# Moving the activation loads of a one-core transformer trunk from SyncE's queue to GpSimd's

## The chip, the cores and the metric

The kernel runs on one core of one Trainium2 chip, as one launch. The metric is the device time of that core in microseconds (us), from the start of the execution to its end. Three runs of the kernel before the change took 2092.64, 2093.26 and 2091.36 us; the median is 2092.64 us.

## The reference, cut to what matters

The reference is a two-layer encoder trunk over 256 positions of 2048 features in float32. The change concerns only how the input `x` reaches the first projection of layer 0:

```python
D_MODEL, SEQ = 2048, 256
HYB_IN_WIDTH = A_WIDTH + 2 * A_KV_WIDTH + 2 * B_WIDTH     # 3584

def reference(x, ...):
    for layer in range(2):
        h = rms_norm(x, mixer_norm_w[layer])
        if layer == 0:
            proj = h @ hyb_w_in[0]          # 2048 x 3584
            ...                             # window attention and gMLP gating
            mixed = concat(attn, sgu) @ hyb_w_out[0]
        else:
            ...                             # qkv, stick-breaking attention
        x = x + mixed
        h = rms_norm(x, ffn_norm_w[layer])
        x = x + (silu(h @ w_gate) * (h @ w_up)) @ w_down
    return x
```

## The kernel before, in words

All matrix products are made of three matmuls on rounded halves of both factors: high part times high part, low part of the activations times high part of the weights, high part of the activations times low part of the weights (L1087, L1088 and L1093). The activations are the stationary side (128 features x 128 positions), the weights the moving side (128 x 512).

Weights stream through a ring. A "unit" is 4 tiles of 128 x 512 (1 MB), loaded into one of 4 slots of `raw` by SyncE (SP). A "half" is 2 of its tiles: ScalarE (ACT) rounds it to `w_hi` (L539), VectorE (DVE) makes `w_lo` from the rest (L742), and TensorE (PE) does its 12 matmuls: 2 position tiles x 2 weight tiles x 3 products. The list HALVES orders all halves of the program, and every engine follows it. SP issues a unit when DVE has finished the unit that had the slot before (semaphore `lo_ready`).

The first chunk of the first projection needs the activations too. The host hands over `xT`, x with features on the partitions, 2 MB. It is loaded into `xT_raw` in six pieces of 2, 2, 2, 2, 4 and 4 feature tiles, `XT_PIECES = [0, 2, 4, 6, 8, 12, KT]`, with a semaphore each (`xt_landed`). Halves 0, 1, 2, 3, 4 and 6 begin with pieces 0 to 5. Before a half that begins with a piece, ACT waits for the piece, scales and rounds its tiles into `xT_hi` (L529), and only then waits for the half's weights and rounds them; DVE makes `xT_lo` (L738), then `w_lo`. PE waits for `xT_lo` of the piece and `w_hi` of the half. So piece 0 stands ahead of everything that PE does, and each later piece ahead of its half.

Below, x0 to x5 are the six pieces (256 KB each for x0 to x3, 512 KB for x4 and x5), w0a and w0b the two halves of unit 0 (512 KB each, loaded apart, L443 and L445), w1a and w1b those of unit 1, and w2 and w3 the next two units whole (1024 KB, L450). SP issues them in the order x0, w0a, x1, w0b, x2, w1a, x3, w1b, x4, w2, x5, w3, and none of these waits for anything. KB and MB are the profile's issue sizes (1 MB is 1024 KB).

While the first loads are on their way, PE runs 14 warm-up matmuls on a tile of ones (WARM_UP, L1233). GpSimd (POOL) sets the ones (L463) and clears a part of `wsT` (L466), then waits until ACT has rounded nine halves, then loads twelve small constants (L469). For the rest of the program it moves the "folds": blocks to DRAM and back.

Of the kernel before, what the change touches and what calls it, by code (L numbers as in the profile page):

```python
# [61 lines left out]
XT_PIECES = [0, 2, 4, 6, 8, 12, KT]  # L62
# [116 lines left out]
def splits(F):  # L179


    return sum(split for split, _ in FOLDS[:F])
# [56 lines left out]
def build(nc, x, xT, normw, w_gate, w_up, w_down, w_in, qkw, sinks, gnw, ws, bs, w_out0, w_qkv, w_out1,  # L239
          ident, dist, tri, strict, out):  # L240
    es = ExitStack()
    with es:
        def sem(name):
            return es.enter_context(nc.semaphore(name))

        def sb(name, shape, dt=F32, ctx=None):
            return (ctx or es).enter_context(nc.sbuf_tensor(name, shape, dt))
# [42 lines left out]
        with ExitStack() as c0:  # L290
# [9 lines left out]
            with ExitStack() as c1:  # L300
                xT_raw = sb("xT_raw", [P, KT, SEQ], F32, c1)
# [33 lines left out]
        xt_landed = [sem(f"xt_landed{q}") for q in range(len(XT_PIECES) - 1)]  # L335
# [52 lines left out]
        def weights(ph, i, c):  # L388

            if ph.name == "in":  # L390
                return w_in, IN_COLS[c]
            if ph.name == "out":
                return (w_out0, w_out1)[ph.layer], c * CH
            if ph.name == "up":
                return (w_gate, w_up)[c][ph.layer], (ph.hidden0 + i) * CH
            if ph.name == "down":
                return w_down[ph.layer], c * CH
            return w_qkv, i * CH + c * C_HEADS * C_DIM
# [29 lines left out]

        @block.sync
        def _(sp):  # L430
            def load_x(piece):
                k0, k1 = XT_PIECES[piece:piece + 2]
                sp.dma_start(xT_raw[:, k0:k1, :], xT[:, k0:k1, :]).then_inc(xt_landed[piece], 16)

            def unit(it, h):
                ph, u = it.ph, h.unit
                w, col = weights(ph, it.i, h.c)
                row = (ph.hidden0 * GRP if ph.name == "down" else 0) + h.k0
                src = w.rearrange("(k p) n -> p k n", p=P)[:, row:row + UNIT, col:col + CH]
                if u < 4:  # L440
                    load_x(u + min(u, 2))
                if u in (0, 1):
                    sp.dma_start(raw[:, u, 0:2, :], src[:, 0:2, :]).then_inc(first_landed[u], 16)  # L443
                    load_x(2 * u + 1)
                    sp.dma_start(raw[:, u, 2:4, :], src[:, 2:4, :]).then_inc(raw_landed[u], 16)  # L445
                    return
                if u >= RING:

                    sp.wait_ge(lo_ready, 2 * (u - RING) + 2)
                sp.dma_start(raw[:, h.raw_slot, :, :], src).then_inc(raw_landed[h.raw_slot], 16)  # L450

            for it, h in HALVES:
                if h.part == 0:
                    unit(it, h)
            for tt in range(TT):
                sp.wait_ge(x_added, 2 * (D // CH) * RESIDUALS - TT + tt + 1)
                sp.dma_start(out[tt * P:(tt + 1) * P, D - CH:], x_sb[:, tt, D - CH:]).then_inc(last_stored, 16)
            sp.wait_ge(last_stored, 16 * TT)


        @block.gpsimd
        def _(pool):
            nc.gpsimd.memset(ones_sb[:], 1.0).then_inc(cleared, 1)  # L463
            pool.wait_ge(cleared, 1)

            nc.gpsimd.memset(wsT[CHUNK:P, :, 0:CHUNK], 0.0).then_inc(cleared, 1)  # L466
            pool.wait_ge(hi_ready, 9)
            for dst, src in SMALL:
                pool.dma_start(dst, src).then_inc(small_landed, 16)  # L469
            def bounce(F):  # L470


                pool.wait_ge(fold_done, F + 1)
                pool.dma_start(blocks.rearrange("t p n -> p t n"), (p_folded if F < A_KV else folded)[:, :, :]).then_inc(fold_out, 16)  # L474
                pool.wait_ge(fold_out, 16 * F + 16)
                if F < A_KV:
                    back = p_spread[:, :, :, :]
                    if F:
                        pool.wait_ge(turned, PH[0].turn(0, IN_TURN[f"o{F - 1}"]) + 1)
                else:  # L480
                    back = spread[:, F % 2, :, :, :]
                    if F >= A_KV + 2:
                        split, g = FOLDS[F - 2]
                        if split:
                            pool.wait_ge(fold_lo, splits(F - 2) + 1)
                        else:
                            pool.wait_ge(qk_split, g)
                for b in range(QUARTERS):
                    pool.dma_start(back[b * BLK:(b + 1) * BLK].rearrange("j t a r -> j (t a) r"),  # L489
                                   blocks[:, :, b * P:(b + 1) * P].rearrange("t (a j) r -> j (t a) r", a=QUARTERS)).then_inc(fold_landed, 16)  # L490
                pool.wait_ge(fold_landed, 16 * QUARTERS * (F + 1))

            for F in range(len(FOLDS)):
                bounce(F)

            base = 2 * (D // CH) * (RESIDUALS - 1)
            for c in range(D // CH - 1):
                pool.wait_ge(x_added, base + 2 * c + 2)
                pool.dma_start(out.rearrange("(t p) d -> p t d", p=P)[:, :, c * CH:(c + 1) * CH],
                               x_sb[:, :, c * CH:(c + 1) * CH]).then_inc(stored, 16)  # L500
            pool.wait_ge(stored, 16 * (D // CH - 1))
# [791 lines left out]
```

## Time and profile before

| | |
|---|---|
| median of 3 runs | 2092.64 us |
| profiled execution, its own time | 2091.34 us |
| its span, first to last instruction | 2089.3 us |
| PE busy | 2080.0 us (100%) |
| DVE busy | 1217.6 us (58%) |
| ACT busy | 973.5 us (47%) |
| POOL busy | 149.8 us (7%) |
| the 16 DMA engines, SP's queue q1 | 392.72 MB, 56.2% |
| POOL's queue q0 | 51.08 MB, 9.3% |
| ACT's queue q10 | 2.13 MB, 0.3% |

The profile is of one execution, whose own time is 1.3 us below the median of the runs. Between its span and its time lie 2.04 us outside the first and the last instruction. Times in the trace count from the first instruction. The share of the chain that ended last is 96% PE: the kernel is bound by matmuls, and all but some microseconds of it are the same 9,420 matmul instructions back to back.

### The profile page before, as it was taken

How to read it: one execution, taken by the hardware profiler on the slowest of the kernel's cores; microseconds unless marked ns; L12 is line 12 of the kernel's file. 1: busy time of each engine (PE TensorE's matmuls, PEld its weight loads, DVE VectorE, ACT ScalarE, POOL GpSimd, SP SyncE). 2: the span in 40 equal slices, each digit the busy share in tenths (PEclk: the TensorE clock that was granted, in tenths of full speed). 3: DMA queues.
4: the chain of work that ended last, by engine and by line, in shares of the span. 5: the costliest groups of instructions: out<-in, count | busy, mean ns of one | idle time of the engine just before them, and what ended most of it. 6: DMA issues, size and time to landing. Idle time of an engine off the chain costs nothing.

```text
span 2089.3 us, 22670 instructions
## 1 busy us (share of the span) xinstructions
PE 2080.0 (100%) x9420; PEld 1723.5 (82%) x9420; DVE 1217.6 (58%) x1298; ACT 973.5 (47%) x1086; POOL 149.8 (7%) x251
## 2 busy tenths in 40 slices
PE   9999999999999999999999999999999999999999
PEld 8877888888888888888888888888888888888887
DVE  7776655555455554556666666656555465554654
ACT  6556554443444434445555455554443444434443
POOL 1010100100001000011110100100100001000010
PEclk9999999999999999999999999999999999999999
DMA  9665776765667656677766666766766567665673
GB/s 334 215 184 180 240 238 207 232 219 194 197 206 232 219 194 198 205 234 245 239 212 206 213 201 197 232 216 217 238 209 201 187 213 238 209 201 187 213 237 129
DMA packets 214566, 447.37 MB, mean 214 GB/s; under 512 B 10224, under 2 KB 10240, under 8 KB 214208
## 3 DMA queue, kind: packets, MB, share of 16 engines
q1 hardware_dynamic: 197600, 392.72, 56.2%
q0 software_dynamic: 16448, 51.08, 9.3%
q10 hardware_dynamic: 416, 2.13, 0.3%
q8 instruction: 74, 1.21, 0.2%
q14 instruction: 28, 0.23, 0.0%
HBM read 419.67 MB, written 26.21 MB: 213 GB/s over the span
## 4 chain that ended last, share of the span: by engine, by line
PE 96%; DVE 2%; ACT 2%; issue 0%; DVEq 0%; POOL 0%; POOLq 0%
PE acc L1087 31%; PE acc L1093 31%; PE acc L1088 31%; DVE w_lo L742 1%; ACT att L653 1%; ACT w_hi L539 0%; PE turn_zb L1206 0%; PE turn_zb L1233 0%; PE turn_zb L1107 0%; PE turn_zb L1146 0%; DVE att L968 0%; DVE att L953 0%; DVE p_folded L791 0%; PE turn_zb L1117 0%; ACT L511 0%
## 5 line engine op out<-in xcount | busy, mean ns | idle before, releaser
L742 DVE TENSOR_TENSOR w_lo<-raw,w_hi 128x1024 fp32r<-128x1024 f32 x744 | 899.5, 1220 | 591.6 <-ACT w_hi L539 591.4
L539 ACT ACTIVATE w_hi<-raw 128x1024 fp32r<-128x1024 f32 x744 | 786.1, 1059 | 982.9 <-PE acc L1093 978.5
L1087 PE MATMUL acc<-w_hi,xT_hi 128*128 128x512 f32 x2016 | 788.1, 391 | 0.7 <-ACT w_hi L539 0.6
L1088 PE MATMUL acc<-w_hi,xT_lo 128*128 128x512 f32 x2016 | 785.8, 390 | 0.0
L1093 PE MATMUL acc<-w_lo,xT_hi 128*128 128x512 f32 x2016 | 539.3, 390 | 0.7 <-DVE w_lo L742 0.7
L1087 PEld LDWEIGHTS acc<-w_hi,xT_hi 128*128 128x128 f32 x2016 | 379.1, 188 | 81.4 <-issue 1.8
L1093 PEld LDWEIGHTS acc<-w_lo,xT_hi 128*128 128x128 f32 x2016 | 378.5, 188 | 79.8 <-DVE w_lo L742 1.5
L1088 PEld LDWEIGHTS acc<-w_hi,xT_lo 128*128 128x128 f32 x2016 | 379.3, 188 | 77.2
L1087 PE MATMUL acc<-w_hi,m_hi 128*128 128x512 f32 x960 | 374.3, 390 | 0.0
L1088 PE MATMUL acc<-w_hi,m_lo 128*128 128x512 f32 x960 | 373.9, 389 | 0.0
L1093 PE MATMUL acc<-w_lo,m_hi 128*128 128x512 f32 x960 | 256.7, 389 | 0.0
L1087 PEld LDWEIGHTS acc<-w_hi,m_hi 128*128 128x128 f32 x960 | 180.3, 188 | 37.5 <-issue 0.2
L1093 PEld LDWEIGHTS acc<-w_lo,m_hi 128*128 128x128 f32 x960 | 180.3, 188 | 37.3
L1088 PEld LDWEIGHTS acc<-w_hi,m_lo 128*128 128x128 f32 x960 | 180.4, 188 | 37.0
L474 POOL DMA_DIRECT2D blocks<-folded x42 | 30.3, 722 | 1556.3 <-DVE folded L791 1355.3
L489 POOL DMA_DIRECT2D spread<-blocks x168 | 97.4, 587 | 162.1 <-DMA blocks<-folded 157.0
L846 DVE TENSOR_TENSOR x_sb<-acc,x_sb 128x512 f32<-128x512 f32 x64 | 41.2, 686 | 81.7 <-PE acc L1093 81.7
L750 DVE TENSOR_SCALAR hid<-acc,rstd 128x512 f32<-128x512 f32 x44 | 31.0, 747 | 58.7 <-PE acc L1093 58.7
L834 DVE SCALAR_TENSOR_TENSOR hid<-acc,rstd,hid 128x512 f32<-128x512 f32 x44 | 31.0, 747 | 58.4 <-PE acc L1093 58.4
L800 DVE TENSOR_TENSOR m_lo<-spread,m_hi 128x1024 fp32r<-128x1024 f32 x22 | 26.8, 1220 | 3.5 <-ACT m_hi L556 3.5
L791 DVE STREAM_TRANSPOSE folded<-hid 128x512 f32<-128x512 f32 x44 | 28.5, 686 | 0.0
L556 ACT ACTIVATE m_hi<-spread 128x1024 fp32r<-128x1024 f32 x22 | 23.0, 1045 | 4.2 <-DMA spread<-blocks 4.2
(149 smaller groups left out, 526.5 us busy)
## 6 DMA issues: line engine op xcount, KB each, us to landing
raw<-in_w_gate SPq DMA_DIRECT2D x88, 1024.0 KB, 5.2
raw<-in_w_up SPq DMA_DIRECT2D x88, 1024.0 KB, 5.9
raw<-in_w_down SPq DMA_DIRECT2D x88, 1024.0 KB, 5.1
raw<-in_w_qkv SPq DMA_DIRECT2D x48, 1024.0 KB, 5.8
raw<-in_w_out SPq DMA_DIRECT2D x32, 1024.0 KB, 5.2
raw<-in_w_in SPq DMA_DIRECT2D x26, 1024.0 KB, 6.1
blocks<-folded POOLq DMA_DIRECT2D x42, 512.0 KB, 4.0
spread<-blocks POOLq DMA_DIRECT2D x168, 128.0 KB, 6.0
```

The costliest lines, as they stand in the source:

```text
L474: pool.dma_start(blocks.rearrange("t p n -> p t n"), (p_folded if F < A_KV else folded)[:, :, :]).then_inc(fold_out, 16)
L489: pool.dma_start(back[b * BLK:(b + 1) * BLK].rearrange("j t a r -> j (t a) r"), blocks[:, :, b * P:(b + 1) * P].rearrange("t (a j) r -> j ...
L539: nc.scalar.activation(w_hi[:, h.slot, :, :], raw[:, h.raw_slot, 2 * h.part:2 * h.part + 2, :], ACTF.Copy).then_inc(hi_ready, 1)
L742: nc.vector.tensor_tensor(w_lo[:, h.slot, :, :], raw[:, h.raw_slot, 2 * h.part:2 * h.part + 2, :], f32(w_hi[:, h.slot, :, :]), ALU.subtrac ...
L750: ins = nc.vector.tensor_scalar(dst[:, tt, :], acc[:, it.pair(c), tt, :], rstd[:, tt:tt + 1], None, ALU.mult)
L791: ins = nc.vector.transpose((p_folded if F < A_KV else folded)[:, tt, :].rearrange("p (b k t) -> p b k t", b=QUARTERS, k=GRP), src[:, tt, ...
L800: ins = nc.vector.tensor_tensor(d, s, f32(h), ALU.subtract)
L834: nc.vector.scalar_tensor_tensor(out=hid[:, tt, :], in0=acc[:, it.pair(1), tt, :], scalar=rstd[:, tt:tt + 1], in1=hid[:, tt, :], op0=ALU.m ...
L846: nc.vector.tensor_tensor(xs, acc[:, it.pair(c), tt, :], xs, ALU.add).then_inc(x_added, 1)
L1087: nc.tensor.matmul(dst, hi[:, h.k0 + k, at], wh, start=h.opens and k == 0, stop=False)
L1088: nc.tensor.matmul(dst, lo[:, h.k0 + k, at], wh, start=False, stop=False)
L1093: ins = nc.tensor.matmul(dst, hi[:, h.k0 + k, at], w_lo[:, h.slot, k, :], start=False, stop=h.closes and k == 1)
```

## The change

The six loads of x leave SP's program and are issued by GpSimd, in the same pieces and order and with the same semaphores, straight after the tile of ones is set and before the part of `wsT` is cleared. SP's queue then holds only the weights.

```diff
         @block.sync
         def _(sp):
-            def load_x(piece):
-                k0, k1 = XT_PIECES[piece:piece + 2]
-                sp.dma_start(xT_raw[:, k0:k1, :], xT[:, k0:k1, :]).then_inc(xt_landed[piece], 16)
-
             def unit(it, h):
...
-                if u < 4:
-                    load_x(u + min(u, 2))
                 if u in (0, 1):
                     sp.dma_start(raw[:, u, 0:2, :], src[:, 0:2, :]).then_inc(first_landed[u], 16)
-                    load_x(2 * u + 1)
                     sp.dma_start(raw[:, u, 2:4, :], src[:, 2:4, :]).then_inc(raw_landed[u], 16)
                     return
...
             nc.gpsimd.memset(ones_sb[:], 1.0).then_inc(cleared, 1)
             pool.wait_ge(cleared, 1)
 
+
+            for piece in range(len(XT_PIECES) - 1):
+                k0, k1 = XT_PIECES[piece:piece + 2]
+                pool.dma_start(xT_raw[:, k0:k1, :], xT[:, k0:k1, :]).then_inc(xt_landed[piece], 16)
             nc.gpsimd.memset(wsT[CHUNK:P, :, 0:CHUNK], 0.0).then_inc(cleared, 1)
```

SyncE's program begins, before the change, with the twelve loads in turn; `xT_raw` is the destination of x, `raw` that of the weights:

```order
L433 DMA xT_raw<-in_xT 128x512
L443 DMA raw<-in_w_in 128x2x512
L433 DMA xT_raw<-in_xT 128x512
L445 DMA raw<-in_w_in 128x2x512
L433 DMA xT_raw<-in_xT 128x512
L443 DMA raw<-in_w_in 128x2x512
L433 DMA xT_raw<-in_xT 128x512
L445 DMA raw<-in_w_in 128x2x512
L433 DMA xT_raw<-in_xT 128x1024
L450 DMA raw<-in_w_in 128x4x512
L433 DMA xT_raw<-in_xT 128x1024
L450 DMA raw<-in_w_in 128x4x512 x25
```

After the change SyncE's program begins so (w0a, w0b, w1a, w1b, then w2, w3 and the units that wait for a slot):

```order
L437 DMA raw<-in_w_in 128x2x512
L438 DMA raw<-in_w_in 128x2x512
L437 DMA raw<-in_w_in 128x2x512
L438 DMA raw<-in_w_in 128x2x512
L443 DMA raw<-in_w_in 128x4x512 x26
```

Six issues are gone from between the weights, which keep their order.

GpSimd's program, before, at its start; the first constants follow the clearing of `wsT`:

```order
L463 MEMSET ones_sb 128x128
L466 MEMSET wsT 64x8x64 [waits cleared]
L469 DMA ident_sb<-in_ident 128x128 [waits hi_ready]
L469 DMA tri_sb<-in_tri 128x128
```

And after the change:

```order
L456 MEMSET ones_sb 128x128
L462 DMA xT_raw<-in_xT 128x512 [waits cleared]
L462 DMA xT_raw<-in_xT 128x512 x3
L462 DMA xT_raw<-in_xT 128x1024 x2
L463 MEMSET wsT 64x8x64
L466 DMA ident_sb<-in_ident 128x128 [waits hi_ready]
L466 DMA tri_sb<-in_tri 128x128
```

The six loads stand between the two memsets. The compute engines' programs are the same as before.

## Rows read from the trace of the kernel before

**Rows 1.** Busy time by stretch (columns: each engine's, granted clock, DMA share, GB/s)

```profile
142.00:149.00 7.00, 4.67 (x22) 4.15 (x22) 6.92 (x11) 3.00 (x7) 0.72 (x1) 0.76 0.65 224
149.00:2086.00 1937.00, 1935.40 (x8672) 1604.81 (x8671) 1107.12 (x1128) 882.73 (x929) 135.29 (x222) 1.00 0.66 212
...
145.00:149.00 4.00, 4.00 (x19) 3.61 (x18) 3.97 (x8) 1.72 (x5) 0.72 (x1) 0.57 0.98 369
```

**Rows 2.** Waits of PE's matmuls: us in total, times, longest

```profile
PE turn_zb L1146 <- DVE m_lo L782: 2.3, 1, 2.3
PE turn_zb L1233 <- POOL ones_sb L463: 1.0, 1, 1.0
PE turn_zb L1107 <- DVE kv L907: 0.8, 1, 0.8
```

**Rows 3.** Timeline of the start: start, us, engine, line; idle before

```profile
0.75 0.39 SPq L433 DMA_DIRECT2D xT_raw<-in_xT  x1
1.00 5.59 PE L1233 MATMUL turn_zb<-ones_sb 128*128 128x128 f32 x28 [1.00 <-POOL ones_sb L463]
1.01 0.52 POOL L466 MEMSET wsT<- 64x512 f32 x1
4.35 0.91 ACT L529 ACTIVATE xT_hi<-xT_raw,normw_sb 128x256 fp32r<-128x256 f32 x2 [1.88 <-DMA normw_sb<-in_normw]
5.44 1.06 ACT L539 ACTIVATE w_hi<-raw 128x1024 fp32r<-128x1024 f32 x1 [0.18 <-DMA raw<-in_w_in]
...
6.59 33.24 SPq L450 DMA_DIRECT2D raw<-in_w_in  x8
...
6.64 0.47 PE L1087 MATMUL acc<-w_hi,xT_hi 128*128 128x512 f32 x1
```

**Rows 4.** Issues of x0, w0a (at 1.19), w0b (2.17), w1b (4.26): us to landing

```profile
xT_raw<-in_xT SPq DMA_DIRECT2D x1, 256.0 KB, 3.3
raw<-in_w_in SPq DMA_DIRECT2D x1, 512.0 KB, 4.2
raw<-in_w_in SPq DMA_DIRECT2D x1, 512.0 KB, 5.4
raw<-in_w_in SPq DMA_DIRECT2D x1, 512.0 KB, 8.3
```

**Rows 5.** Timeline at half 1 and at half 4

```profile
9.26 0.19 PEld L1087 LDWEIGHTS acc<-w_hi,xT_hi 128*128 128x128 f32 x1
...
16.56 2.01 ACT L539 ACTIVATE w_hi<-raw 128x1024 fp32r<-128x1024 f32 x2 [1.01 <-DMA raw<-in_w_in]
...
17.73 0.19 PEld L1087 LDWEIGHTS acc<-w_hi,xT_hi 128*128 128x128 f32 x1 [0.35 <-issue]
```

**Rows 6.** Timeline of POOL: its first two DMA issues

```profile
26.16 0.70 POOL L469 DMA_DIRECT2D ident_sb<-in_ident  x1 [24.63 <-ACT w_hi L539]
26.85 0.55 POOL L469 DMA_DIRECT2D tri_sb<-in_tri  x1
```

**Rows 7.** POOL's DMA issues of the whole trace: KB each, median us to landing

```profile
blocks<-folded POOLq DMA_DIRECT2D x42, 512.0 KB, 4.0
...
gnw_sb<-in_gnw POOLq DMA_DIRECT2D x1, 512.0 KB, 6.6
wsT<-in_ws POOLq DMA_DIRECT2D x1, 256.0 KB, 6.9
...
ident_sb<-in_ident POOLq DMA_DIRECT2D x1, 64.0 KB, 5.0
```

**Rows 8.** DMA packets by queue: in 26.1 to 29 us, then 284 to 285.5

```profile
DMA packets 556, 1.11 MB, mean 381 GB/s; under 512 B 16, under 2 KB 16, under 8 KB 556
q1 hardware_dynamic: 556, 1.11, 103.3%
...
q0 software_dynamic: 103, 0.42, 68.2%
q1 hardware_dynamic: 104, 0.21, 36.4%
```

## The prediction

> **What bounds the kernel now.** I read the page's busy shares first, then the busy time by stretch, the waits of PE, the timeline of the first 20 us, and last the DMA issues and the packets of each queue. From 149 to 2086 us PE is busy for 1935.40 of 1937 us [rows 1]. No load of x is in that stretch, so nothing that the change does can be gained or lost there, except as a shift of the whole. The waits of PE say the same: the one long one is 2.3 us at L1146, in the attention part, and the 1.0 us ahead of the warm-up is the tile of ones [rows 2]. What can change is when PE begins and whether it is fed in its first eight halves.
>
> The start is a chain. SP issues x0 at 0.75, ACT begins to round it at 4.35 (it is released by the norm weights, which come 0.3 us after x0), rounds w0a from 5.44 to 6.50, and PE begins at 6.64 [rows 3]. PE has been busy with the warm-up until 6.59, so two things end together: the chain of x0 and w0a, and the warm-up. Neither has slack: an x0 that is 1 us late is seen nearly whole, one that is early is worth nothing. From there PE runs without a gap, with one exception: at half 4 it waits 0.35 us, since w2 came late, and ACT stood idle for it for 1.01 us [rows 5].
>
> **What the change does, and the sum.**
>
> SP loses six issues. They cost it some 0.5 us each, so w3, issued at 6.59 [rows 3], is issued at about 3.5. That alone brings PE nothing, except at half 4: the 0.35 us there can go if weights come no later than now. I take -0.35 us when x doesn't crowd them, 0 as the other bound.
>
> POOL gains six issues of 0.55 us, the first perhaps 0.70 [rows 6]: 3.5 us, from 1.01, where the clearing of `wsT` starts now [rows 3]. Then comes that clearing, 0.52 us, done at about 5. Behind it stands the wait for the ninth rounded half, in which POOL idles for 24.63 us until 26.16 [rows 6]. So the issue time on POOL is hidden with 20 us to spare, and folds come after that. Cost 0. PE's tile of ones is set before, at its old place. Without this cover it would be 3.5 us on whoever waits for POOL.
>
> x0 is the term that counts. It is issued at 1.01 instead of 0.75, and its landing takes what POOL's queue takes. The lower bound is SP's own 3.3 us [rows 4], landing at 4.3: nothing lost, since ACT starts at 4.35 for the norm weights anyway. The upper bound is the 256 KB of `wsT`, 6.9 us [rows 7], landing at 7.9; there 512 KB of the same queue stood ahead. Between lie 4.0 us for 512 KB to DRAM, mostly with little beside them, and 5.0 us for 64 KB of `ident` [rows 7], which was the first DMA on POOL's queue and met a backlog of weights, as x0 will. The backlog is visible: POOL issued `ident` at 26.16, and in 26.1 to 29 us 556 packets moved, all of them of SP's queue [rows 8]. x0 meets less of it, because SP has begun only 0.26 us before, but x0 is four times as large as `ident` and shares with w0a and w0b. I take 5.5 us, nearest to `ident` with some transfer on top: x0 lands at 6.5.
>
> The Trainium skill, page "DMA: Bandwidth & Descriptors", section "Latency and other measured facts", gives about 1 us to the first byte for GpSimd's path and about 0.6 us for the other. By that alone x0 would be 0.26 + 0.4 us later and the sum about +0.6 us; the trace's 5.0 us for 64 KB stands far above it, so the measured row decides.
>
> From x0's landing on, the rows give the rest: 0.91 us for `xT_hi`, 1.06 for `w_hi`, and 0.14 from there to PE's start (6.50 to 6.64) [rows 3], 2.11 us; w0a is there by then. PE begins at 6.5 + 2.11 = 8.6, 2.0 us later than now. x1 to x5 follow 0.55 us apart by issue, and each has a half of PE time, 2.7 us, to come. Weights w0b and w1 come earlier than now or about as now. So PE isn't stopped again, and the 0.35 us at half 4 is swallowed: 2.0 - 0.35 = +1.6 us.
>
> **The clock** adds a term. PE stands idle for 2.0 us between the warm-up's end at 6.59 and 8.6. Once in this trace it was idle for as long, the 2.3 us ahead of L1146 [rows 2]; after it the granted clock from 145 to 149 us was 0.57 [rows 1]. That is 3.4 of the 4 us at 1.2 GHz instead of 2.4 (1 - 0.57 = 0.43, times 4, over 0.5), with 1.7 us of work lost, as PE was busy throughout. Whether an idle time of 2.0 us at this place brings the same the trace can't say: bounds 0 and 1.7, and I take the middle, 0.9.
>
> Sum: +2.0 - 0.35 + 0.9 = +2.5 us. On the profiled execution that is 2091.34 + 2.5 = 2093.8; its own time is 1.3 us below the median of the runs, so on the median it is 2092.64 + 2.5, **2095.1 us**, or +0.12%. The smallest difference that a measurement of this kernel can tell from none is about 0.2%, 4.2 us.
>
> **The rivals.**
>
> *Crowding, +3.5 to +6 us.* Where both queues have a backlog they alternate packet by packet, and POOL's are larger: 103 packets with 0.42 MB against 104 with 0.21 [rows 8]. If that holds from the start, x takes two thirds of the rate until its 2 MB are through, and weights one third. Now 1.5 MB have landed when w0b does, at 2.17 + 5.4 = 7.57, and 3 MB when w1b does, at 4.26 + 8.3 = 12.56 [rows 4]. Crowded, w0a is done when 1.5 MB are through (about 7.2 with its head start), and w0b when 3 MB are, at about 12 to 12.6. Then half 1 starts at 12 + 1.06 + 0.14 = 13.2 to 13.8, against 9.26 now [rows 5]: +3.9 to +4.5, less 0.35. PE idles twice, so a clock step of 1.7 may be added. Against it: at the start SP is ahead, and its first 1 MB may be in the engines before x0 is. Time about 2097.
> The same page, section "Queues, rings and completion order", states that each DMA engine goes round robin over the queue rows at packet granularity. By that rule this rival is what happens; the trace agrees in the stretch quoted, and disagrees in 26.1 to 29 us, where one queue had everything.
>
> *x0 behind the weights, +4.5 to +8 us: slower.* If POOL's first packets wait as those of `ident` did, but for everything that SP issues in its first 2 us (w0a to w1b, 2 MB), x0 lands with 2.25 MB through. At (12.56 - 7.57) / 1.5 = 3.3 us per MB from w0b's landing on that is 7.57 + 0.75 x 3.3 = 10.0, and PE begins at 12.1: +5.5, less 0.35, and with a clock step +6.9. The point from which it decides: the total passes 4.2 us when x0 lands after 6.64 + 4.2 + 0.35 - 2.11 = 9.1, or after 7.4 with one clock step. For it: `ident`'s rows. Against it: x0 is issued 0.26 us after w0a and ahead of w1a. Time about 2098.5.
>
> *Hidden anyway, -0.35 to +0.5 us.* x0 lands by 4.6, since the DMA engines are empty then. ACT starts as now, the warm-up covers the rest, and half 4 no longer waits. A gain can't be larger: PE can't begin before 6.59, and there is one gap of 0.35. For it: 4.0 us for twice the bytes [rows 7]. Time 2092.6.
>
> **How the numbers follow.** The forecast (x0 late by some 2 us, with or without a clock step) 0.50; crowding 0.23; x0 behind the weights 0.13; hidden 0.14. Slower by over 0.2% are about half of the crowding (0.11) and most of the third (0.11): 0.22. Faster by over 0.2% needs 4 us that aren't there to be won: 0.02, for what I don't see. Within: 0.76. The range goes from 2092.3, the hidden case with the lower half of the runs' own spread of 2 us cut off, to 2098.5, the crowding with a clock step and half of the third rival. Outside stay about half of the hidden case and half of the third, 0.14, and some chance for a spread of the runs larger than that seen, 0.05.
>
> **What would show it.** On the timeline: x0's issue by POOL at about 1.0 and ACT's first `xT_hi` at about 6.5, released by x; PE's first product at about 8.6; half 4 without its wait; the granted clock in the first 20 us; the stretch of the middle unchanged. Wrong it would be if ACT starts at 4.35 as before, if ACT waits for w0b rather than for x (crowding), or if x0 lands after 9. A change of more than 1 us behind 30 us would mean that something is moved that I hold to be still.

## The result and the profile after

The median after the change is 2095.23 us (2093.41 to 2099.09 in 22 runs); the kernel before, in 22 runs beside it, has 2091.36 us (2089.81 to 2093.4). The ratio is 1.0018, with a 95% interval of 1.0012 to 1.0023: 3.9 us more, just inside the 0.2% (4.2 us) that the prediction took as its bound, and clear of zero. The profiled execution has a span of 2092.9 us and a time of 2094.93, each 3.6 us above the profiled execution of before.

The page's line of busy times after. PE's differs by 0.7 us from before, so no work was added; what was lost is waiting and clock:

```profile
PE 2079.3 (99%) x9420; PEld 1721.3 (82%) x9420; DVE 1216.8 (58%) x1298; ACT 973.0 (46%) x1086; POOL 153.0 (7%) x257
```

The timeline of the start after. It answers to [rows 3]: start, us, engine, line, and in brackets the idle time before.

```profile
0.75 0.44 SPq L437 DMA_DIRECT2D raw<-in_w_in  x1
...
1.00 4.75 PE L1230 MATMUL turn_zb<-ones_sb 128*128 128x128 f32 x28 [1.00 <-POOL ones_sb L456]
...
1.32 3.36 POOL L462 DMA_DIRECT2D xT_raw<-in_xT  x6 [0.37 <-POOL ones_sb L456]
...
4.72 0.52 POOL L463 MEMSET wsT<- 64x512 f32 x1
7.27 0.91 ACT L526 ACTIVATE xT_hi<-xT_raw,normw_sb 128x256 fp32r<-128x256 f32 x2 [4.78 <-DMA xT_raw<-in_xT]
8.08 1.04 ACT L536 ACTIVATE w_hi<-raw 128x1024 fp32r<-128x1024 f32 x1
...
9.27 0.47 PE L1084 MATMUL acc<-w_hi,xT_hi 128*128 128x512 f32 x1 [3.52 <-ACT w_hi L536]
...
10.74 0.63 PE L1084 MATMUL acc<-w_hi,xT_hi 128*128 128x512 f32 x1
```

ACT is now released by x, where the norm weights released it before. It begins at 7.27, 2.92 us later than in [rows 3], and PE's first product is at 9.27, 2.63 us later. `w_hi` follows without a wait, so w0a had landed before (3.9 us after its issue, at about 4.7). The last row shows the clock: the same matmul that took 0.40 us a moment before takes 0.63.

The DMA issues of 0.9 to 1.5 us, KB each, us to landing; they answer to [rows 4]:

```profile
raw<-in_w_in SPq DMA_DIRECT2D x2, 512.0 KB, 4.4
xT_raw<-in_xT POOLq DMA_DIRECT2D x1, 256.0 KB, 5.9
```

So x0 took 5.9 us where SP's had taken 3.3. The packets say why. From 3.1 to 4.9 us, with x0 issued at 1.32, one packet in 364 was POOL's; from 8 to 13 us the queues went one for one, and POOL's packets were the larger (1.29 MB in 369 against 0.71 MB in 372):

```profile
DMA packets 364, 0.71 MB, mean 396 GB/s; under 512 B 17, under 2 KB 17, under 8 KB 364
...
q1 hardware_dynamic: 363, 0.71, 102.5%
q0 software_dynamic: 1, 0.00, 0.6%
...
q0 software_dynamic: 369, 1.29, 66.3%
q1 hardware_dynamic: 372, 0.71, 37.2%
```

The busy time by stretch after (columns: each engine's, granted clock, DMA share, GB/s):

```profile
10.50:14.00 3.50, 3.50 (x10) 2.77 (x9) 3.50 (x6) 2.92 (x6) 0.00 (x0) 0.53 1.03 400
...
149.00:2086.00 1937.00, 1935.33 (x8678) 1603.81 (x8677) 1109.67 (x1133) 884.35 (x933) 136.01 (x223) 1.00 0.66 213
```

The clock was granted at 0.53 from 10.5 to 14 us: nearly all of it at 1.2 GHz instead of 2.4. The second row is the long stretch of [rows 1], and by its sum it is as before to 0.1 us. In the attention part one more stretch, and from the timeline the matmul that waits there:

```profile
140.00:160.00 20.00, 17.37 (x110) 13.74 (x110) 15.96 (x27) 11.41 (x23) 3.04 (x5) 1.00 0.65 213
```

```profile
148.49 2.02 PE L1143 MATMUL turn_zb<-gs,wsT 128*128 128x128 f32 x16 [2.35 <-DVE m_lo L779]
```

The wait of 2.3 us of [rows 2] is still there (L1143 is what was L1146, by then 4.0 us later), but no stretch at half rate follows: the clock is 1.00 over all 20 us, where [rows 1] have 0.57 in 145 to 149. PE's waits after:

```profile
PE acc L1084 <- ACT w_hi L536: 4.1, 3, 3.5
PE turn_zb L1143 <- DVE m_lo L779: 2.3, 1, 2.3
...
PE acc L1084 <- DVE xT_lo L799: 0.5, 1, 0.5
PE turn_zb L1114 <- DVE kT_lo L992: 0.2, 1, 0.2
```

The last two weren't in the trace of before.

### The profile page after: what moved, and what is told of

It reads as the page before. It is cut to its first block, busy times and chain, and to the rows that moved or that the text cites. A ratio compares the mean times of both kernels' runs of the same rounds, so it can differ in the third digit from the quotient of the medians.

```text
span 2092.9 us, 22670 instructions
## 1 busy us (share of the span) xinstructions
PE 2079.3 (99%) x9420; PEld 1721.3 (82%) x9420; DVE 1216.8 (58%) x1298; ACT 973.0 (46%) x1086; POOL 153.0 (7%) x257
## 3 DMA queue, kind: packets, MB, share of 16 engines
q8 instruction: 74, 1.21, 0.2%
## 4 chain that ended last, share of the span: by engine, by line
PE 92%; DVE 3%; ACT 2%; DMA 2%; issue 1%; POOL 0%; DVEq 0%; POOLq 0%
PE acc L1084 30%; PE acc L1090 30%; PE acc L1085 30%; DVE w_lo L739 1%; DMA spread<-blocks 1%; DMA blocks<-folded 1%; ACT att L650 1%; ACT w_hi L536 0%; DMA xT_raw<-in_xT 0%; PE turn_zb L1203 0%; POOL spread L486 0%; PE turn_zb L1104 0%; DVE att L965 0%; DVE att L950 0%; PE turn_zb L1114 0%
```

## The experiments

Seven further kernels ran, and before and after were profiled twice more each. For each profile the start of PE's matmuls was compared with the same matmuls of the first profile of before, and the table gives the shift in us at five places: the first product, just ahead of the wait at 145 us (all of the start is in it), 200 us, 1006 us (the last weights of layer 0), and the end. "Idle" is PE's idle time ahead of the first product, "at 1.2 GHz" the stretches in which the granted clock was at its lower level. Left out are the warm-up, for which the trace has no granted clock (see the last section), and a stretch at the very end that every profile has.

| kernel | idle | first product | 145 | 200 | 1006 | end | at 1.2 GHz |
|---|---|---|---|---|---|---|---|
| before, second profile | 0.0 | -0.12 | +0.15 | +0.09 | +0.27 | +0.45 | 145.7-149.1 |
| before, third | 0.0 | +0.03 | -0.09 | -0.10 | -0.10 | -0.18 | 145.8-149.2 |
| after, first | 3.5 | +2.63 | +4.0 | +2.35 | +3.2 | +3.55 | 10.7-14.1 |
| after, second | 1.8 | +2.46 | +3.8 | +2.2 | +3.03 | +2.95 | 10.5-13.9 |
| after, third | 3.0 | +2.52 | +5.0 | +3.4 | +3.74 | +3.91 | 8.2-15.0 |
| x on ACT's queue | 2.0 | +2.23 | +3.6 | +2.0 | +2.8 | +2.71 | 9.7-13.1 |
| only x0 on POOL | 1.1 | +1.81 | +1.57 | +1.56 | +1.56 | +1.48 | 147.1-150.5 |
| x0 on SP | 0.0 | +0.20 | +2.25 | +2.19 | +3.52 | +4.11 | 146.6-150.0 |
| x0 queued first | 4.7 | +4.29 | +6.0 | +5.99 | +5.99 | +6.21 | 8.2-15.1, 151.6-155.0 |
| after, WARM_UP 26 | 0.0 | +2.69 | +2.45 | +0.79 | +0.79 | +5.02 | 1067.7-1071.1 |
| after, WARM_UP 22 | 1.2 | +2.51 | +2.27 | +2.25 | +2.25 | +4.34 | 148.1-151.5 |
| before, WARM_UP 26 | 0.0 | +1.65 | +1.41 | -0.19 | -0.19 | +1.45 | none |

**Is it the clock at the start?** A longer warm-up, in the kernel after, covers PE's idle time and leaves the queues alone.

```diff
-WARM_UP = 14
+WARM_UP = 26
```

> The changed kernel with 26 warm-up matmuls instead of 14, so that TensorE is busy nearly until x0 is ready; nothing else moves. In the profile of the changed kernel TensorE idled for 3.52 us before its first product at 9.27, and the granted clock then fell for 3.4 us (1.7 us of work lost). Theory: the idle time brings the clock step; here the first product still comes at 9.2 to 9.4, no half-rate stretch follows in the first 30 us, and the time is 2.2 to 2.6 us over the kernel before instead of 3.9. Rival: the step has another cause (a matter of chance at the start); then it is seen here too and the time stays 3.5 to 4.3 us over.

The first product came where it came after (9.33 us), no step of the clock followed, neither at the start nor at 145, and at 200 us the shift was only +0.79. But the median is 2096.0 us, 1.0023 [1.0014, 1.0032], where 2.2 to 2.6 us more than before was expected. In its profile more than had been saved was lost near 1066 us, in a wait of PE for `kT_lo`, followed by a step of the clock:

```profile
PE turn_zb L1114 <- DVE kT_lo L992: 2.4, 1, 2.4
```

So the step of the clock at the start is a true cost there (+2.45 at 145 us without it, +4.0 with it), and taking it away didn't bring the time back in this kernel.

**Is POOL's queue slow in itself?** The same loads, issued by ACT behind its load of the norm weights:

```diff
-                pool.dma_start(xT_raw[:, k0:k1, :], xT[:, k0:k1, :]).then_inc(xt_landed[piece], 16)
...
+                act.dma_start(xT_raw[:, k0:k1, :], xT[:, k0:k1, :]).then_inc(xt_landed[piece], 16)
```

> The six loads of x are issued by ScalarE straight after the norm weights, so from a second queue as in the change, but not from GpSimd's. Order theory (what is queued first goes first, whichever queue): x0 is issued some 0.45 us after w0a and about when w0b is, and lands after w0a and part of w0b, at 5.2 to 6.5; first product at 7.3 to 8.6; time +0.7 to +2 us over the kernel before. Path theory (GpSimd's queue is slow in itself, the order of the two queues matters little): x0 lands within 3.3 to 3.7 us of its issue, at 4.5 to 4.9, first product at 6.7 to 7.0, and the time is within 0.7 us of the kernel before.

The issue of x0, 256 KB, and its us to landing, in this kernel:

```profile
xT_raw<-in_xT ACTq DMA_DIRECT2D x1, 256.0 KB, 5.6
```

It is 0.3 us better than on POOL's queue. ACT issued until 4.98 us and loaded its table from 5.01 to 6.29, both ahead of x0's landing at 6.83. The median is 2093.74 us, 1.0013 [1.0005, 1.0022], an interval that overlaps with that of after. A second queue of the same kind as SP's makes x0 nearly as late, a little later than even the order theory had it (first product at 8.87 us, 7.3 to 8.6 expected).

**Only x0 on POOL's queue.** Before, with one load moved; SP keeps x1 to x5.

```diff
-                if u < 4:
+                if 0 < u < 4:
                     load_x(u + min(u, 2))
...
+            pool.dma_start(xT_raw[:, 0:XT_PIECES[1], :], xT[:, 0:XT_PIECES[1], :]).then_inc(xt_landed[0], 16)
```

> The kernel before with x0 alone issued by GpSimd; x1 to x5 stay in SyncE's queue between the weights. If the loss of the change is x0's landing, all of it stays: x0 lands at 6.5 to 7.5, first product at 8.6 to 9.5, a clock step is likely, and the time is 3 to 4.5 us over the kernel before. If the loss is that x as a whole crowds the weights out (rival), nearly all goes: within 1 us of the kernel before.

The issue of x0, and from the timeline PE's first product:

```profile
xT_raw<-in_xT POOLq DMA_DIRECT2D x1, 256.0 KB, 5.1
```

```profile
8.45 0.47 PE L1088 MATMUL acc<-w_hi,xT_hi 128*128 128x512 f32 x1 [1.13 <-ACT w_hi L540]
```

This is the shift of x0 with little else: +1.81 at the first product, +1.48 at the end, and the later path was as before. The median is 2092.92 us, 1.001 [1.0002, 1.0019]: +2.1 by the ratio, +1.4 by the two medians (before had 2091.48 in the runs beside it). Expected were 3 to 4.5 us with a step of the clock; PE idled for 1.1 us, and no step came at the start.

**All but x0 on POOL's queue.** After, with x0 back on SP ahead of the weights.

```diff
+            sp.dma_start(xT_raw[:, 0:XT_PIECES[1], :], xT[:, 0:XT_PIECES[1], :]).then_inc(xt_landed[0], 16)
             for it, h in HALVES:
...
-            for piece in range(len(XT_PIECES) - 1):
+            for piece in range(1, len(XT_PIECES) - 1):
```

> The changed kernel with x0 back at the head of SyncE's queue, x1 to x5 on GpSimd's. If the loss is x0's landing: x0 lands at 4.1, first product at 6.6 to 6.8, no long idle time of TensorE and no clock step in the first 30 us; x1 is the next in question, issued at 1.3 and landing at 6.5 to 8, which its half needs by about 7.0: a wait of up to 1 us at half 1. Time between -0.4 and +1.2 us against the kernel before. If x as a whole crowds the weights: w0b and w1a late, waits of 2 us or more in halves 1 to 3, +2 to +4 us.

Timeline of this kernel: ACT and PE at halves 0 to 2.

```profile
6.84 0.47 PE L1085 MATMUL acc<-w_hi,xT_hi 128*128 128x512 f32 x1
...
7.52 0.91 ACT L527 ACTIVATE xT_hi<-xT_raw,normw_sb 128x256 fp32r<-128x256 f32 x2 [0.99 <-DMA xT_raw<-in_xT]
...
9.64 1.06 ACT L537 ACTIVATE w_hi<-raw 128x1024 fp32r<-128x1024 f32 x1 [1.21 <-DMA raw<-in_w_in]
...
10.84 0.47 PE L1085 MATMUL acc<-w_hi,xT_hi 128*128 128x512 f32 x1 [0.99 <-ACT w_hi L537]
...
13.40 1.06 ACT L537 ACTIVATE w_hi<-raw 128x1024 fp32r<-128x1024 f32 x1 [1.91 <-DMA raw<-in_w_in]
...
14.61 0.47 PE L1085 MATMUL acc<-w_hi,xT_hi 128*128 128x512 f32 x1 [0.80 <-ACT w_hi L537]
```

PE begins as before, and is then stopped twice because the weights are late: ACT stands 0.99 us for x1 and then 1.21 us for w0b, and 1.91 us for w1a. This is the rival that the prediction called crowding, bare. It costs 2.0 us from the first product to 145 (+0.20 to +2.25). The median is 2093.34 us, 1.0009 [1.0, 1.0018], an interval that reaches down to no difference; its profiled execution (2095.38) was the longest of the eleven, so its +4.11 at the end is above its median.

**x0 with nothing ahead.** After, with SP held until POOL has issued x0.

```diff
+            sp.wait_ge(cleared, 2)
             for it, h in HALVES:
...
                 pool.dma_start(xT_raw[:, k0:k1, :], xT[:, k0:k1, :]).then_inc(xt_landed[piece], 16)
-            nc.gpsimd.memset(wsT[CHUNK:P, :, 0:CHUNK], 0.0).then_inc(cleared, 1)
+                if piece == 0:
+                    nc.gpsimd.memset(wsT[CHUNK:P, :, 0:CHUNK], 0.0).then_inc(cleared, 1)
```

> The changed kernel, with SyncE's weights held until GpSimd has issued x0 and cleared its part of wsT behind it (that clearing moves up to behind x0's issue), so x0 is queued ahead of all weights; x1 to x5 follow. Order theory: x0 lands within 3.6 to 4.2 us of its issue, at 4.9 to 5.5, instead of 5.9 us after it; but w0a, issued at about 2.6, now lands at 7 to 9 among x1 to x3 and the first product comes at 8.2 to 10. Path theory (GpSimd's queue is slow in itself): x0 still lands at 6.9 to 7.4. The total is no better than the changed kernel's in either: +3 to +6 us.

The issue of x0, and from the timeline ACT's first two steps:

```profile
xT_raw<-in_xT POOLq DMA_DIRECT2D x1, 256.0 KB, 3.1
```

```profile
4.47 0.91 ACT L528 ACTIVATE xT_hi<-xT_raw,normw_sb 128x256 fp32r<-128x256 f32 x2 [2.01 <-DMA xT_raw<-in_xT]
...
9.73 1.06 ACT L538 ACTIVATE w_hi<-raw 128x1024 fp32r<-128x1024 f32 x1 [4.35 <-DMA raw<-in_w_in]
```

On POOL's queue the same 256 KB took 3.1 us, less than SP's 3.3 [rows 4]. Now w0a was the late one: issued at 2.62 beside x1 to x5, it landed 7.1 us later. The median is 2098.11 us, 1.0031 [1.0019, 1.0043], at the upper end of the +3 to +6 us expected or over it (+6.5 by the ratio, from 5 runs).

**A warm-up of 22.** After, with a shorter lengthening, to see whether the late loss comes from it.

> The changed kernel with 22 warm-up matmuls, so that the warm-up surely ends before x0 is ready, unlike with 26, where it ended at 9.51 us. If the surplus of the long warm-up (2096.0 us at the median) came from a late event that is part of chance (a wait of 2.4 us for kT_lo near 1065 us and the clock step behind it), this kernel is at +2.3 to +3.9 us, its product begins at 9.2 to 9.4 and no half-rate stretch follows. If more warm-up costs time in itself, it is again at +4.4 or more.

PE was idle for 1.2 us, and no step of the clock followed at the start; the one at 145 was back. The late wait came again, 1.9 us. The median is 2096.99 us, 1.0028 [1.0018, 1.0038]: by what was set down ahead of the run, the case in which a longer warm-up costs time in itself (+4.4 or more), and not the case of chance. POOL's timeline shows where the wait comes from (`blocks` are the folds' blocks in DRAM, `spread` where they are read back to), first of this kernel:

```profile
1051.87 0.72 POOL L471 DMA_DIRECT2D blocks<-folded  x1 [7.00 <-DMA spread<-blocks]
1060.65 2.47 POOL L486 DMA_DIRECT2D spread<-blocks  x4 [8.05 <-DMA blocks<-folded]
```

and then of the kernel after:

```profile
1051.75 0.72 POOL L471 DMA_DIRECT2D blocks<-folded  x1 [5.91 <-DMA spread<-blocks]
1056.40 2.47 POOL L486 DMA_DIRECT2D spread<-blocks  x4 [3.93 <-DMA blocks<-folded]
```

One write of `blocks` that keeps POOL 8.05 us instead of 3.93 delays the reading back by 4.2 us, and `kT_lo`, which is made from what is read back, comes late for PE, which had some slack there. Why that write takes longer in one profile than in the other, this doesn't say.

**The queues of before, PE late.** WARM_UP 26 in the kernel before: PE starts 1.65 us late, and no DMA is moved.

> The kernel before with 26 warm-up matmuls: TensorE's first product comes at about 9.5 as in the changed kernel, but all queues are as before and TensorE is never idle there. If the rest of the changed kernel's loss (its waits near 1003 and 1063 us) comes from beginning later, the same waits of 0.3 to 4 us appear here, and the time is 3 to 5 us over the kernel before. If it comes from the queues, none appears: the start is 2.7 to 2.9 us late, 0.35 us of that is given back at half 4, the total is +2.3 to +2.6 us.

There was no step of the clock anywhere, and at 200 us the kernel was 0.19 us ahead of before. Then the same wait, 1.4 us:

```profile
PE turn_zb L1117 <- DVE kT_lo L995: 1.4, 1, 1.4
```

The median is 2095.06 us, 1.0019 [1.001, 1.0028], although the profiled execution, 2092.66, was the shortest of its 11 runs. So a kernel with the queues as they were, but a longer warm-up and a later start, ends about as far off as the change does. This doesn't show that the late start does it: "only x0 on POOL" starts as late (+1.81, +1.56 at 200 us) with 14 warm-up matmuls and had no such wait. A wait for `kT_lo` of 1.4 us or more came in the three profiles with a longer warm-up and in none of the ten with 14 (0.4 us at most). What the longer warm-up has to do with it, if anything, is open.

**The spread between profiles.** Before and after were profiled twice more each, unchanged.

> The kernel before, profiled a second time. If the clock step near 145 us and the absence of waits of TensorE near 1003 and 1063 us belong to the kernel, all are as in the first profile. If they are chance, the step may be missing or stand elsewhere, and waits of 0.2 to 2.4 us for xT_lo or kT_lo may be there.

> The changed kernel, profiled a second time. First product at 9.2 to 9.4 again and x0 landed 5.7 to 6.1 us after its issue, since those follow from the order of the queues. The clock step behind the start and the waits near 1003 and 1063 us: again if they belong to the kernel, changed if they are chance.

> The kernel before, profiled a third time. If what two profiles showed is the kernel's own: step of the clock near 146 us, none at the start, waits near 1003 and 1063 us of 0 to 0.2 us. Otherwise they are chance.

> The changed kernel, profiled a third time. If what two profiles showed is its own: first product at 9.1 to 9.3, step of the clock at 10.5, none near 146 us, about 0.8 us lost near 1003 us. Otherwise they are chance.

They took 2091.84 and 2091.19 us (before), 2094.17 and 2095.12 us (after). The table has their shifts: both repeats of before lie within 0.5 us of its first profile; after has the step at the start and none at 145 in all three, and differs by 1.2 us in what the step costs and by 0.2 in where the first product stands.

## Why the prediction was right, and where it was off

The prediction said 2095.1 us, and 2095.23 was measured. The sum of +2.5 us was made on the profiled execution and carried to a median of 2092.64. The 22 runs of before have a median 1.3 us lower, so the difference is 3.9 us: the sum was 1.4 us short, and the agreement to 0.1 us is luck. What was right are the sign and the first term. On the profiled executions the terms stand thus:

| term | forecast | profile after |
|---|---|---|
| x0 late, to the first product | +2.0 | +2.63 |
| wait at half 4 | -0.35 | -0.24 |
| clock | +0.9 | +1.6 at the start, -1.65 at 145 |
| late waits | 0 | +0.85 near 1003, +0.35 near 1063 |
| sum | +2.5 | +3.55 |

**x0 is the term that counts: right.** It landed at 7.2 us where 6.5 was said: the issue is at 1.32 instead of 1.01, and the landing took 5.9 instead of 5.5. The 2.11 us from there to PE's start measured 2.0 (7.27 to 9.27). "Only x0 on POOL" carries the term by itself to the end: +1.48 in its profile, +1.4 by its median or +2.1 by its ratio.

**Why it is late: the backlog, as in the row of `ident`, and not the kind of queue.** Three runs tell this: 3.1 us on POOL's queue with nothing ahead, 5.9 on the same queue behind w0a and w0b, 5.6 on ACT's behind the same. In the kernel after x0 had one packet moved by 4.9 us, 3.5 us after its issue; with nothing ahead its first packets moved at 2.7 us, 1.4 us after its issue (14 of them by 3.2 us). Until 4.9 us SP's queue moved 0.91 MB, which is most of w0a and w0b, issued at 0.75 and 1.24. So the third rival's mechanism was the true one, but for 1 MB ahead, not for the 2 MB with which I priced it; x0 landed ahead of the 7.4 us from which it would have decided.

**The page's rule on arbitration.** The Trainium skill, page "DMA: Bandwidth & Descriptors", section "Queues, rings and completion order", has each DMA engine go round robin over its queue rows. The trace agrees from 8 to 13 us (369 packets against 372) and not from 3.1 to 4.9 (1 against 363), though x0 had been issued at 1.32; from 5 to 8 us it was 165 against 268.

**Crowding: a true mechanism, hidden by the late start.** From 8 to 13 us x took 66% of the engines' time and the weights 37%. After the late x0, ACT still waited 0.91 us for w1b, but PE was by then slowed and late, and did not stop. With PE on time, in "x0 on SP", the same crowding costs 2.0 us. Within the start the two do not add: up to 145 us, x0 alone on POOL costs 1.57 and the rest without x0 2.25, together 3.8, but both at once 4.0 less the 1.6 of the clock, 2.4. The whole runs can't settle it: 2.1 and 1.9 by the ratios, 1.4 and 1.9 by the medians, against 3.9 for both, each with an interval of some 1.9 us to either side, and the late waits are in them.

**The clock: right at the place, wrong as a sum.** The step came, near its upper bound of 1.7 (3.4 us at half rate, some 1.6 us of work; 6.8 us in the third profile). What I left out is that the step at 145, which before has, might go when one comes at the start. In all three profiles of after, and with x on ACT's queue, a step at the start went with none at 145, though PE idled the same 2.3 us there. The net was 0, or +1.1 in the third profile (2.75 at the start less 1.65), which came near the forecast of 0.9 only in that one. Shown is that the two went together in these four; "x0 queued first" had both, and WARM_UP 26 had neither, so it isn't a rule, and why stays open.

**"The stretch of the middle unchanged": wrong by 0.5 to 1.2 us.** The sum put this term at nothing. Busy time by stretch hides it, since the stretch moves with the shift. The shift grows behind 200 us by 1.2 us in the first profile, 0.75 in the second, 0.5 in the third, by 0.36 and -0.08 in before's two. It grows at waits for folds that pass through DRAM. In the first profile of after, POOL stood 6.30 us for `blocks` ahead of the read back at 992 us, against 4.93 us in before. That figure alone decides nothing: with WARM_UP 26 before had 6.86 there and PE lost nothing. Whether the change causes more of these is not settled: the kernel before with a longer warm-up, whose queues are untouched, has them as well (1.4 us), and its ratio is the change's (1.0019 against 1.0018). That a start shifted against the stream of weights meets these transfers otherwise would account for both, but no run here shows it, and "only x0 on POOL" speaks against it: it starts 1.56 us late and lost nothing behind 200 us (+1.48 at the end). By the table, a growth between 200 and 1006 us of more than 0.2 us (0.35 to 1.33) came in five of the eight profiles with x1 to x5 off SP's queue and in none of the other five, so the queues may have a part in that piece; it isn't shown. No kernel started late without either a moved load or a longer warm-up. So of the 3.55 us of the first profile the 2.35 up to 200 us are accounted for, and the other 1.2 are only placed.

**Hidden at no cost: right for POOL.** Its six issues took 3.36 us (3.5 was said), the clearing of `wsT` was done at 5.24 us, and the wait for the ninth half still covered 21.56 us:

```profile
26.80 0.54 POOL L466 DMA_DIRECT2D ident_sb<-in_ident  x1 [21.56 <-ACT w_hi L536]
```

And there was nothing to be won: PE can't start before its warm-up ends, and the one gap of 0.35 us is all that earlier weights could close.

## What to carry to other kernels

A second queue gives no second place at the head: here a small load issued 0.6 us behind 1 MB on another queue waited until the DMA engines were nearly through with that, whichever engine issued it. So whatever the first product needs last goes first on the queue that starts first, and the split between queues is judged by who lands first, and not by how evenly the issues are spread. When a start moves, carry the shift through the whole trace at four or five places: here the clock gave back at 145 us what it took at 10 (in two profiles of three), and waits at 1003 and 1063 us added a part that the sums by stretch don't show.

## What the runs showed of the hardware beyond that

- **Bytes, not packets, are unequal.** Once both queues had a backlog they alternated one for one, and as POOL's packets carried some 3.5 KB and SP's 1.9 KB on average (1.29 MB in 369, 0.71 MB in 372), x took two thirds of the rate.
- **Idle time and the clock.** At the start 1.8, 2.0, 3.0, 3.5 and 4.7 us of idle time each went with a stretch at 1.2 GHz, begun in the idle time or behind it, of 3.4 to 6.9 us; 1.1 and 1.2 us did not. At 145 us the same idle of 2.3 us was followed by one in 7 of the 13 profiles and not in 6.
- **The warm-up has no fixed length.** The same 14 matmuls took 4.75 us in one profile of after, 5.59 in before and 6.32 with only x0 on POOL. The views print a clock of 1.00 there, but the trace's record of the granted clock begins only at 3.9 us in the first of these, 5.65 in the second and 7.2 in the third, and the matmuls tell the rest: in all 13 profiles they start 0.21 us apart at first and 0.11 us apart from within 0.2 us of that moment on (in two profiles, where it comes behind the warm-up, 0.21 us to the end): half the rate, then the full one. So the warm-up begins at 1.2 GHz in every profile, and its length goes by when the clock rises, at 3.9 to 7.2 us. Below are 5 to 7 us of two profiles, both with the warm-up running throughout: only x0 on POOL with 11 instructions, and WARM_UP 22 with 20, both printed as 1.00. PE's idle time behind the warm-up was 3.5 us in one profile of after and 1.8 in another for this reason, with the first product within 0.2 us. What makes the clock rise earlier or later is open.

```profile
5.00:7.00 2.00, 2.00 (x11) 2.00 (x10) 0.00 (x0) 0.55 (x2) 0.00 (x0) 1.00 1.02 390
```

```profile
5.00:7.00 2.00, 2.00 (x20) 2.00 (x19) 0.00 (x0) 0.00 (x0) 0.23 (x1) 1.00 1.05 378
```
